# Expert blocks of 120 token slots in place of 128, and one 2 MB transfer for gate and up weights in place of two

## The reference

```python
grp = jnp.argmax(g_logits, axis=-1)                  # one of 4 groups
top_p, top_i = lax.top_k(jax.nn.softmax(e_logits, axis=-1), TOP_K)   # 2 of its 8 experts
eid = grp[:, None] * EXPERTS_PER_GROUP + top_i       # 32 experts, 2176 pairs
def expert_block(args):
    xblk, e = args
    hid = jax.nn.silu(xblk @ w_gate[e]) * (xblk @ w_up[e])    # 1024 -> 256
    return hid @ w_down[e]                                    # 256 -> 1024
# y[token] += weight * expert_block(rows of that expert)
```

## Time and profile before

| | us |
|---|---|
| median of 3 runs | 1272.56 (1270.76 to 1273.21) |
| profiled execution, its own time | 1273.04 |
| its span, first to last instruction | 1271.4 |
| PE busy | 1228.9 |
| DVE busy | 1036.4 |
| ACT busy | 705.8 |
| experts: first transposes to last result | 972.97 to 1261.2 |

### The profile page before, as it was taken

One profiled execution on the slowest core, in us unless ns is written; L12 is line 12 of the kernel. 1 busy time (PEld: TensorE's weight loads), 2 busy tenths in 40 slices (PEclk: granted clock), 3 DMA queues, 4 the chain that ended last, 5 costly groups with the idle time before them and its releaser, 6 DMA issues. The chain is left out here.

```text
span 1271.4 us, 28372 instructions
## 1 busy us (share of the span) xinstructions
PE 1228.9 (97%) x11174; PEld 821.8 (65%) x11174; DVE 1036.4 (82%) x1479; ACT 705.8 (56%) x1160; POOL 311.5 (25%) x280
## 2 busy tenths in 40 slices
PE   7899999998999999999999999999998999999995
PEld 5456666665666666666665666655555888888884
DVE  5777777776989999999999676535756999999993
ACT  5656666666443452354343664423222899999983
POOL 1383111111010010011000000000134367667663
PEclk9999999998999999999999999999999999999998
DMA  9700000033141442244141145547678999999982
GB/s 349 173 10 3 1 0 0 3 122 101 56 110 54 125 111 76 84 127 110 36 137 51 52 143 202 173 172 278 235 235 307 321 391 386 391 398 384 387 307 48
DMA packets 53081, 211.34 MB, mean 166 GB/s; under 512 B 14560, under 2 KB 15776, under 8 KB 40416
## 3 DMA queue, kind: packets, MB, share of 16 engines
q1 hardware_dynamic: 31888, 156.95, 33.1%
q0 software_dynamic: 18672, 44.42, 14.4%
q10 hardware_dynamic: 2448, 8.98, 1.8%
HBM read 180.98 MB, written 39.72 MB: 174 GB/s over the span
## 5 line engine op out<-in xcount | busy, mean ns | idle before, releaser
L1396 DVE SCALAR_TENSOR_TENSOR big<-c_region,c_taps,big 128x1024 f32<-128x1024 f32 (+1 forms) x120 | 153.4, 1279 | 3.7 <-ACT caT L1087 3.7
L74 PE MATMUL c_psb<-xnT,w_taken 128*128 128x364 f16 x456 | 145.5, 319 | 0.0
L75 PE MATMUL c_psb<-xnT,w_taken 128*128 128x364 f16 x456 | 145.5, 319 | 0.0
L1396 DVE SCALAR_TENSOR_TENSOR caT<-c_region,c_taps,caT 128x1024 f32<-128x1024 f32 x112 | 143.2, 1278 | 0.0
L2095 POOL DMA_INDIRECT y_all<-o_hn,e_idx_y x29 | 91.9, 3168 | 38.8 <-POOL e_idx_y L2091 23.3
L74 PE MATMUL c_psa<-xnT,w_taken 128*128 128x364 f16 x312 | 99.8, 320 | 0.1
L75 PE MATMUL c_psa<-xnT,w_taken 128*128 128x364 f16 x312 | 99.8, 320 | 0.0
L74 PE MATMUL o_psH<-big,e_gu 128*128 128x128 f16 x512 | 87.4, 219 | 0.8 <-DVE big L2442 0.8
L75 PE MATMUL o_psH<-big,e_gu 128*128 128x128 f16 x512 | 87.4, 219 | 0.0
L76 PE MATMUL o_psH<-big,e_gu 128*128 128x128 f16 x512 | 87.4, 219 | 0.0
L76 PE MATMUL c_psb<-xnT,f_w_l_first 128*128 128x364 f16 x240 | 76.2, 317 | 0.0
(11 more groups left out here) (437 smaller groups left out, 3977.2 us busy)
## 6 DMA issues: line engine op xcount, KB each, us to landing
e_gu<-w_gu SPq DMA_DIRECT2D x28, 1024.0 KB, 12.0
w_taken<-w_feat SPq DMA_DIRECT2D x48, 512.0 KB, 4.1
e_d<-w_dn SPq DMA_DIRECT2D x15, 1024.0 KB
o_room<-w_gu SPq DMA_DIRECT2D x12, 1024.0 KB
xnT<-w_gu SPq DMA_DIRECT2D x12, 1024.0 KB
big<-w_gu SPq DMA_DIRECT2D x12, 1024.0 KB
c_region<-gates POOLq DMA_DIRECT2D x8, 1092.0 KB, 5.8
xnT<-w_dn SPq DMA_DIRECT2D x6, 1024.0 KB
```

The costliest lines, as they stand in the source:

```text
L74: pe.matmul(out, stat[0], mov[0], start=start, stop=False)
L75: pe.matmul(out, stat[0], mov[1], start=False, stop=False)
L1396: dve.scalar_tensor_tensor(y_j, glu[:, p, j:j + SEQ], tap, y_j, op0=ALU.mult, op1=ALU.add).then_inc(tap_done, 1)
```

## The change

- BLK is 120 in place of 128, and NOV 18 in place of 16. xT, hT, the products and the transposes have 120 columns or rows. The gathers and scatters keep 128 indices; the last eight hold T in every block.
- The division of a rank by 120 and by 30 is made by a multiplication with 2185 and shifts.
- Gate and up lie in one array w_gu with rows of 16 KB. For blocks 4, 5 and 9 to 27 they land by one transfer of 2 MB (`load_gate_up`), which waits for both low parts five blocks before; both cuts wait for the one semaphore. The other blocks keep the two halves.

```diff
-BLK = 128
-NOV = 16
+BLK = 120
+NOV = 18
-LANES, LANE_BITS = 4, 5
+LANES = 4
+LANE = BLK // LANES
+PER_LANE, PER_LANE_BITS, LANES_BITS = 2185, 16, 2
...
+        WHOLE = (4, 5) + tuple(range(9, STATIC))
+
+        def buffer_of(b):
+
+            return (0, 1, 0, 1, 2, 3, 4)[b] if b < 7 else (b - 7) % 5
+
+        def landed(b, half):
+
+            f = buffer_of(b)
+            loads = [n for n in range(b + 1) if buffer_of(n) == f]
+            if b in WHOLE or half == 0:
+                return gu_ld[f][0], 16 * len(loads)
+            return gu_ld[f][1], 16 * len([n for n in loads if n not in WHOLE])
...
-                sp.dma_start(gu32[f][:, halves[half]], A[("w_gu0", "w_gu1")[half]][b].rearrange("p (k n) -> p k n", k=HK)
-                             ).then_inc(gu_ld[f][half], 16)
+                sp.dma_start(gu32[f][:, halves[half]], A["w_gu"][b][:, half * HALF:(half + 1) * HALF].rearrange(
+                    "p (k n) -> p k n", k=HK)).then_inc(gu_ld[f][half], 16)
+
+            def load_gate_up(b, f, used=0):
+                if used:
+                    sp.wait_ge(gu_low[0], used)
+                    sp.wait_ge(gu_low[1], used)
+                sp.dma_start(gu32[f], A["w_gu"][b].rearrange("p (k n) -> p k n", k=KC)).then_inc(gu_ld[f][0], 16)
...
-            load_expert(4, 2, 0)
+            load_gate_up(4, 2)
+            load_down(4, 2)
...
-                load_up(b, (b - 7) % 5, 0, b - 4)
-                load_up(b, (b - 7) % 5, 1, b - 4)
+                load_gate_up(b, (b - 7) % 5, b - 4)
                 load_down(b - 1, (b - 8) % 5, b - 5)
...
-                act.activation(xT_h[:, p], psT[:], ACT.Copy, scale=S_X).then_inc(xT_high, 1)
+                act.activation(xT_h[:, p], psRows, ACT.Copy, scale=S_X).then_inc(xT_high, 1)
...
-                act.activation(y_o[:, p], psY, ACT.Copy, scale=weight(b)).then_inc(y_out, 1)
+                act.activation(y_o[0:BLK, p], psY, ACT.Copy, scale=weight(b)).then_inc(y_out, 1)
...
-                done(dve.tensor_copy(rank_i[:, :, a:b], rank[:, :, a:b]))
-                done(dve.tensor_scalar(level[:, :, a:b], rank_i[:, :, a:b], 7, None, ALU.arith_shift_right))
-                done(dve.tensor_scalar(rank_i[:, :, a:b], rank_i[:, :, a:b], LANE_BITS, None, ALU.arith_shift_right))
+                done(dve.tensor_scalar(rank_i[:, :, a:b], rank[:, :, a:b], float(PER_LANE), None, ALU.mult))
+                done(dve.tensor_scalar(level[:, :, a:b], rank_i[:, :, a:b], PER_LANE_BITS + LANES_BITS, None, ALU.arith_shift_right))
+                done(dve.tensor_scalar(rank_i[:, :, a:b], rank_i[:, :, a:b], PER_LANE_BITS, None, ALU.arith_shift_right))
...
-                    last = pe.transpose(psT[:, k, :], xg[:, p, k * P:(k + 1) * P], g.ident[:])
+                    last = pe.transpose(psRows[:, k], xg[0:BLK, p, k * P:(k + 1) * P], g.ident[0:BLK, 0:BLK])
...
-        "c_iota": np.broadcast_to(np.concatenate([np.arange(P).reshape(LANES, P // LANES).T.reshape(-1), np.arange(NE)])
+        "c_iota": np.broadcast_to(np.concatenate([np.arange(BLK).reshape(LANES, LANE).T.reshape(-1), np.full(P - BLK, -1), np.arange(NE)])
```

More of the change, by code:

```diff
@@ L1779, in ffn_phase @@
         xg = xnT_f[:, rest:rest + 2 * D].rearrange("p (a n) -> p a n", a=2)
-        sg, hid = (xnT_f[:, rest + 2 * D + i * DE:rest + 2 * D + (i + 1) * DE].rearrange("p (k n) -> p k n", k=2) for i in range(2))
+        sg, hid = (xnT_f[:, rest + 2 * D + i * DE:rest + 2 * D + (i + 1) * DE].rearrange("p (k n) -> p k n", k=2)[:, :, 0:BLK]
+                   for i in range(2))
         hT = xnT_f[:, rest + 2 * D + 3 * DE:rest + 2 * D + 4 * DE].bitcast(F16).rearrange("p (a k n) -> p a k n", a=2, k=2)
-        hT_h, hT_l = hT[:, 0], hT[:, 1]
-        lastT_h, lastT_l = (big_f[:, rest:rest + 2 * D].bitcast(F16).rearrange("p (b a k n) -> p b a k n", b=2, a=2, k=KC)[:, a, 0, 0:2]
+        hT_h, hT_l = hT[:, 0, :, 0:BLK], hT[:, 1, :, 0:BLK]
+        lastT_h, lastT_l = (big_f[:, rest:rest + 2 * D].bitcast(F16).rearrange("p (b a k n) -> p b a k n", b=2, a=2, k=KC)[:, a, 0, 0:2, 0:BLK]
                             for a in range(2))
         xT = big_f[:, rest:rest + 2 * D].bitcast(F16).rearrange("p (b a k n) -> p b a k n", b=2, a=2, k=KC)
-        xT_h, xT_l = xT[:, 0], xT[:, 1]
+        xT_h, xT_l = xT[:, 0, :, :, 0:BLK], xT[:, 1, :, :, 0:BLK]
         pairs = big_f[:, rest + 2 * D:rest + 2 * D + 2 * NBLK].rearrange("p (b a) -> p b a", a=2)
@@ L1864, in ffn_phase @@
         psL = psN[:, 2 * P:2 * P + RP]
-        psG = [bank[:, 0:DE].rearrange("p (j n) -> p j n", j=2) for bank in (psH[:, 0, 0:512], psH[:, 0, 512:D])]
-        psU = [bank[:, 0:DE].rearrange("p (j n) -> p j n", j=2) for bank in (psM, psN)]
-        psY = psH[:, 1]
+        psG = [bank[:, 0:DE].rearrange("p (j n) -> p j n", j=2)[:, :, 0:BLK] for bank in (psH[:, 0, 0:512], psH[:, 0, 512:D])]
+        psU = [bank[:, 0:DE].rearrange("p (j n) -> p j n", j=2)[:, :, 0:BLK] for bank in (psM, psN)]
+        psY = psH[0:BLK, 1]
+        psRows = psT[:, :, 0:BLK]
         r_ld, rb_ld, gain_ld, iota_ld, upper_ld, unused_st = (
@@ L1897, in ffn_phase @@
         STATIC = 4 * ROUNDS + 8
+        HALF = HK * GU
         BATCHES = ((0, 4), (4, 7), (7, TT))
@@ L1900, in ffn_phase @@
         MARKS = (1, 3, 6)
+        WHOLE = (4, 5) + tuple(range(9, STATIC))
[7 more added lines that the diff above has]
+            return gu_ld[f][1], 16 * len([n for n in loads if n not in WHOLE])
         def staged(b):
[L1904 to L1907, removed]
+            return buffer_of(b), (landed(b, 0), landed(b, 1)), 16 * len([n for n in range(b + 1) if buffer_of(n) == buffer_of(b)])
         def staged_up(q, v):
-            return q + 1, 16 * v + (32 if q == 0 else 16)
+            f = q + 1
+            loads = [n for n in range(STATIC) if buffer_of(n) == f]
+            halved = [n for n in loads if n not in WHOLE]
+            return f, tuple((gu_ld[f][half], 16 * v + 16 * (len(of) + 1 - ROUNDS)) for half, of in enumerate((loads, halved)))
         def staged_down(q, v):
-            return q, 16 * v + (32 if q < 2 else 16)
+            return q, None, 16 * v + (32 if q < 2 else 16)
         def token(b):
@@ L1920, in weight @@
         def weight(b):
-            return pairs[:, ds(b, 1), 1]
+            return pairs[0:BLK, ds(b, 1), 1]
         def rounds(eng):
@@ L2024, in load_up_any @@
                     sp.dma_start(gu32[f][:, halves[half]].rearrange("p k n -> p (k n)"),
-                                 A[("w_gu0", "w_gu1")[half]][ds(e, 1)].rearrange("a p n -> (a p) n")).then_inc(gu_ld[f][half], 16)
+                                 A["w_gu"][ds(e, 1)].rearrange("a p n -> (a p) n")[:, half * HALF:(half + 1) * HALF]).then_inc(gu_ld[f][half], 16)
             def load_down_any(b, f):
@@ L2154, in cut @@
             def cut(load, p, half):
-                f, need = load
-                act.wait_ge(gu_ld[f][half], need)
+                f = load[0]
+                act.wait_ge(*load[1][half])
                 act.activation(gu_h[:, p, halves[half]], gu32[f][:, halves[half]], ACT.Copy,
@@ L2160, in cut_down @@
             def cut_down(load, p):
-                f, need = load
+                f, _, need = load
                 act.wait_ge(d_ld[f], need)
@@ L2400, in control_groups @@
                 dve.wait_ge(l_mm, TT)
[L2401 to L2404, removed]
+                done(dve.tensor_scalar(cnt[:, 0], psC[0:1], 1.0, float(BLK - 1), ALU.max, ALU.add))
+                done(dve.tensor_scalar(cnt_i[:, 0:NE], cnt[:, 0], float(PER_LANE), None, ALU.mult))
+                done(dve.tensor_scalar(cnt_i[:, 0:NE], cnt_i[:, 0:NE], PER_LANE_BITS + LANES_BITS, None, ALU.arith_shift_right))
+                done(dve.tensor_scalar(cnt[:, 0], cnt_i[:, 0:NE], 1.0, None, ALU.subtract))
                 done(dve.tensor_tensor_scan(cnt[:, 1], one[:], cnt[:, 0], 0.0, ALU.mult, ALU.add))
@@ L2441, in rows @@
                 dve.wait_ge(xT_high, b + 1)
-                dve.scalar_tensor_tensor(xT_l[:, p], psT[:], S_X, xT_h[:, p], op0=ALU.mult,
+                dve.scalar_tensor_tensor(xT_l[:, p], psRows, S_X, xT_h[:, p], op0=ALU.mult,
                                          op1=ALU.subtract).then_inc(xT_low, 1)
@@ L2825, in layout @@
         "w_rt": np.concatenate([w_grp, np.zeros((D, 8 - NG), f), w_router], 1).reshape(KC, P, RP).transpose(1, 0, 2),
-        "b_rt": np.concatenate([b_grp, np.full(8 - NG, NEG, f), b_router]), "w_gu0": gu[:, :, 0:gu.shape[2] // 2], "w_gu1": gu[:, :, gu.shape[2] // 2:], "w_dn": dn,
+        "b_rt": np.concatenate([b_grp, np.full(8 - NG, NEG, f), b_router]), "w_gu": gu, "w_dn": dn,
         "c_ident": np.eye(P, dtype=f), "c_bucket": c_bucket, "c_mask": c_mask,
-        "c_iota": np.broadcast_to(np.concatenate([np.arange(P).reshape(LANES, P // LANES).T.reshape(-1), np.arange(NE)])
+        "c_iota": np.broadcast_to(np.concatenate([np.arange(BLK).reshape(LANES, LANE).T.reshape(-1), np.full(P - BLK, -1), np.arange(NE)])
```

5 lines of the change are left out of this document (2 added, 3 removed).

## The result

| | before | after |
|---|---|---|
| median of 6 runs | 1271.67 us (1270.73 to 1273.21) | 1285.46 us (1282.86 to 1286.61) |
| ratio | | 1.0099, 95% interval 1.0088 to 1.0110 |
| span of the profiled execution | 1271.4 us | 1285.0 us |

The account below looks back on a forecast made before the run. PE sets the pace, with the DMA engines a near second limit. Against 1273.04 us profiled: -3.7 early blocks, +12.5 slow blocks, -1.1 last blocks, -2 tail, total +5.7: 1278 us, range 1265 to 1286.

Parts of the forecast that it names:

- Matmuls and the 8.45 us of PE: Expert stage on PE: 96 matmuls of 8 columns fewer save 0.32 us, transposes 0.05; PE then needs 8.45 us a block.
- The load of hT: Before the down projection: loading 120 stationary columns in place of 128 costs 0 to +0.05 us a block, taken as 0.
- DVE and ACT: Expert stage: DVE saves 0.10 us and needs 8.39 us a block, under PE's 8.45; ACT, with 0.68 us idle, follows.
- q0 falls behind and ACT's result waits for the scatter: Indirect queue alternates with load rows packet by packet; scatters come late by up to 1.7 us, delaying ACT's result of block b+2.
- q0 needs 10.5 us a block: Indirect queue: 17.8 packets each wait for a load row of mean 469 ns, plus 2.19 us of its own.
- the work limit that I set beside it (9.7): DMA engines: total work of 9.7 us a block after the change, with 622 ns for a 16 KB row.
- The case "1293": Worse than forecast: q0 at its full 10.5 us for 16 blocks, +20 us; chance 0.08 together with another round.
- A block of 9.6 us, 622 ns a row: Slow blocks of the expert stage taken at 9.6 us for 8.82; a 16 KB load row at 622 ns.
- The scatter loop of 9.35 us: ACT's result to scatter issue 4.5 us, then 11.4 + 2.8 to land, over two blocks: 9.35 us a block.
- 10 blocks at the compute's pace, 16 slow, 3 fast: Expert stage: about 10 blocks at -0.37 each, -3.7; 16 at 9.6 for 8.82, +12.5; the last 3, -1.1 us.
- The spare of 1.8 us: Scatter landing before ACT's result needs its y_o half: 1.8 us to spare, of which two shorter blocks take 0.74.
- The weights' end (rival, 0.22): The last weights, not q0, set the end: -3 us, 1270 (1266 to 1273); chance 0.22.

Follow-up runs that it names:

- experiments 2 to 4: Changed kernel with blocks of 128 slots: 1284.91 us; with 8 KB rows in one 2 MB transfer: 1271.02 us; with scatters of rows 0 to 63 only: 1262.74 us.
- experiment 3: Changed kernel with each gate and up still one 2 MB transfer, but its source laid out so that every row is 8 KB: 1271.02 us, ratio 0.9994.
- experiment 1: Changed kernel, blocks of 120 slots, with gate and up of every expert loaded by two transfers with 8 KB rows: 1272.19 us, ratio 1.0001.
- Experiment 10: Kernel of experiment 1 with the slots' partitions shifted by 8 groups, to load the DMA engines more evenly: 1266.65 us, ratio 0.9965.
- experiment 12: Kernel of experiment 1 with blocks of 128 slots and the slots' partitions shifted by 8 groups: 1271.29 us, ratio 1.0002.

## Why the prediction was right in direction and too small

- **Matmuls and the 8.45 us of PE**: right. Rows start 1.04/20 = 52 ns apart (21 rows, first and last shown), the down projection's still 216, and without a wait the block is 8.46:

```profile
1232.38 0.22 PE L76 MATMUL o_psN<-big,e_gu 128*128 128x120 f16 x1
...
1233.42 0.22 PE L78 MATMUL o_psN<-big,e_gu 128*128 128x120 f16 x1
1233.48 0.38 PE L76 MATMUL o_psH<-e_d,xnT 128*120 128x512 f16 x1
...
1235.86 0.38 PE L78 MATMUL o_psH<-e_d,xnT 128*120 128x512 f16 x1
1236.07 0.99 PE L2633 MATMUL o_psT<-ident,xnT 120*128 120x120 f32 x8
```

- **The load of hT**: taken as 0, and it was. Its weight loads did get longer, from 98 ns to 133, and stay hidden under matmuls 216 ns apart:

```profile
L77 PEld LDWEIGHTS o_psH<-e_d,xnT 128*120 128x120 f16 x106 | 14.1, 133 | 6.6
```

The rule of the Trainium skill (TensorE: Matmul & The Clock Gate, Weight-path perf modes), that the fast load wants all 128 columns, fits this row. The 100 ns that the prediction worked out for such a load do not: the trace has 133. The cost behind it did not come, as one block of 8.46 shows.

- **DVE and ACT**: right. DVE's turn of the rows is 1154 ns for 960 elements (1219 before), and neither sets the pace.
- **q0 falls behind and ACT's result waits for the scatter**: right, by the waits and by experiments 2 to 4. The turns of single packets are borne out by the links in the trace file (2667 of 2672 before). The Trainium skill's turns of whole packets of 9 to 17 descriptors (DMA: Bandwidth & Descriptors, Queues, rings and completion order) do not describe what these rows show: by them the row size should hardly matter, and it is worth 13 us.
- **q0 needs 10.5 us a block**: too much. I took the mean of the load rows alone. q1 has small packets as well, 3511 - 3124 = 387, about 2 an engine in a block, and a turn behind one of those costs nearly nothing. With 3511 packets in 0.786 x 1920 us a turn costs 0.430 us on average, and 17.8 x 0.430 + 2.2 = 9.9 is then the most that q0 can need. It is nothing else than the whole DMA work of a block, so q0's limit and the work limit that I set beside it (9.7) are one. The case "1293" has no ground.
- **A block of 9.6 us, 622 ns a row**: a little too small. The row of 16 KB took 641 ns on average (median 611), so there was hardly a gain in bytes: 8 x 0.019 = 0.15 us a block, and the block was 9.75. My bounds (566 to 632) took for granted that a longer row can't cost more than two.
- **The scatter loop of 9.35 us**: both of its terms were mis-sized, and the errors cancel in part, by luck. Rows of after, ACT's results two blocks apart and the scatter between them:

```profile
1125.69 1.11 ACT L2213 ACTIVATE o_hn<-o_psH,big 120x1024 f32<-120x1024 f32 x1 [1.99 <-DMA y_all<-o_hn,e_idx_y]
...
1127.85 1.60 POOL L2119 DMA_INDIRECT y_all<-o_hn,e_idx_y  x1 [0.93 <-POOL e_idx_y L2115]
...
1145.20 1.11 ACT L2213 ACTIVATE o_hn<-o_psH,big 120x1024 f32<-120x1024 f32 x1 [2.01 <-DMA y_all<-o_hn,e_idx_y]
```

From the result to the issue it is 2.2 us, not 4.5, and from there to the next result but one 17.3, not 11.4 + 2.8 = 14.2. I had counted the scatter's own 9 turns alone; the gathers stand in the same queue, and they too take longer to land, 15.4 us where experiment 3 has 9.2. 19.5 us over two blocks is 9.75 each: the loop closes.

- **10 blocks at the compute's pace, 16 slow, 3 fast**: it was 6, 18 and 5. The spare of 1.8 us was gone at about 1035, soon after the 16 KB rows became continuous. By the turns of the two traces: 18 blocks at +0.93 are +16.7 (forecast +12.5); 11 at -0.36 are -4.0 (forecast -4.8); the first two turns +0.3; the tail from the last turn on -0.6 (forecast -2); the first turn +1.3, of which experiment 1 says why it may be chance or the 120 slots. Sum +13.7; the spans differ by 13.6. Of the 8 us that the forecast lacked, 4.2 lie in the slow blocks' number and length, 1.4 in the tail, 0.8 in the fast blocks and 1.6 at the start.
- **The weights' end (rival, 0.22)**: wrong for the change, right for its half. With 8 KB rows it is what stops the gain of the short blocks (experiment 1), at 1272.2 instead of 1270. I had named its spare as 3 to 5 us. It came out as 0. A good part of it is that the slots of 120 load the DMA engines unevenly: I had priced that at "some 4 us in all" and left it out of the sum. Experiment 10 gives 5.5 us back by the medians, 4.6 by the ratios. That agrees with the Trainium skill's map of partitions to engines (DMA: Bandwidth & Descriptors, The descriptor swizzle), by which two engines lose half of their token rows; no view here shows single engines, so the map is supported by these times alone (with 128 slots, in experiment 12, the same layout brings nothing).
- **What I did not see**: the DMA engines are full for the whole stage in all versions (a share of 1.00 to 1.03 from 1060 to 1180). Before the change the lag went into weight buffers and cost nothing. The change moved it into the queue with only two buffers, y_o.

## What to carry to other kernels

When two DMA queues share full engines, ask which of them may be late, and by how many buffers: longer rows in one queue take time from the other, even though the bytes stay the same. Where a block's DMA work is more than its compute (here 9.7 us against 8.8), shortening the compute brings nothing until the DMA work, on the fullest engine, is less. In this kernel indirect transfers were best at full width, with the filled slots spread over the partitions.

## What the runs showed of the hardware

- Where both queues have packets waiting, an engine takes one of each in turn, whatever their sizes: before the change 2667 of 2672 packets of the indirect queue, rows of 4 KB and packets of 4 and 8 bytes alike, were followed by one of the load queue. Equal counts over a long stretch (3511 to 3530) are no sign of it.
- A row's price goes nearly with its bytes on full engines: 161, 314 and 641 ns on average for 4, 8 and 16 KB.
- Indirect transfers of 120 and 112 rows make all rows dearer: 357 and 361 GB/s at a full share, against 380 with 128 rows. Unexplained.
